# Where the weight stream lands: four raw buffers against the low halves of an eight-slot ring, in a two-layer decoder trunk

## The reference

```
xn = rmsnorm(h); q,k,v,cb,cc,cu,pu,gates = split(xn @ w_in)       # 1024 x 6656
att  = stick_breaking_attention(rmsnorm(q), rmsnorm(k), v)         # 8 heads x 64
conv = cb * causal_conv3(cc * cu);  pool = scale * group_linear(window_mean(pu) - pu)
h += (sum_j sigmoid(gates_j) * (branch_j @ w_branch_j)) @ w_out
h += peer(rmsnorm(h))        # 16384 one-neuron experts: top 16 of each of 8 heads
h += sigmoid(rmsnorm(h) @ w_ple_gate) * (p @ w_ple_proj)
```

## Time and profile before

| | us |
|---|---|
| median of 3 timed runs | 3993.78 (3993.38 to 3993.9) |
| the profiled execution | 3999.43 |
| its span, first to last instruction | 3997.5 |
| PE busy in it | 3923.6 |
| DVE busy | 2696.9 |
| ACT busy | 1453.8 |
| POOL busy | 1305.6 |

### The profile page before, as it was taken

The page is one execution under the profiler, slowest core; times in us unless marked ns, Lnnn a source line. Parts: engine busy times, 40 slices in busy tenths (PEclk is TensorE's granted clock), DMA queues, the critical chain, the costliest instruction groups (busy, mean ns, idle before and its releaser), DMA issues.

```text
span 3997.5 us, 57499 instructions
## 1 busy us (share of the span) xinstructions
PE 3923.6 (98%) x18154; PEld 3235.6 (81%) x18154; DVE 2696.9 (67%) x4417; ACT 1453.8 (36%) x1925; POOL 1305.6 (33%) x887
## 2 busy tenths in 40 slices
PE   8999999999999999999999999999999999999997
PEld 5777888888888878888767778888888888788886
DVE  6753649967774278778577546498777732888785
ACT  5433333333333333333444333333333333333334
POOL 1100003433331077666101000044333401767651
PEclk9999999999999999999999999999999999999999
DMA  3222223445454599999212223234445446999992
GB/s 112 74 84 90 100 86 129 147 161 187 173 184 147 192 338 367 353 350 346 106 68 75 89 90 106 80 137 145 172 176 189 169 147 206 348 371 357 353 332 74
DMA packets 323761, 740.32 MB, mean 185 GB/s; under 512 B 30496, under 2 KB 161696, under 8 KB 319904
## 3 DMA queue, kind: packets, MB, share of 16 engines
q1 hardware_dynamic: 104400, 381.73, 26.8%
q10 hardware_dynamic: 174160, 222.40, 16.5%
q0 software_dynamic: 45056, 134.38, 9.0%
HBM read 618.87 MB, written 119.54 MB: 185 GB/s over the span
## 4 chain that ended last, share of the span: by engine, by line
PE 94%; issue 2%; DVE 2%; ACT 1%; POOL 1%; DMA 0%; ACTq 0%; DVEq 0%; POOLq 0%; SPq 0%
PE bank L1180 61%; PE bank L1395 24%; PE bank L1375 4%; PE bank L1242 1%; PE bank L1232 1%; PE bank L1250 1%; ACT hi L439 0%; PE bank L1325 0%; PE bank L1324 0%; PE bank L1227 0%; PE bank L1323 0%; DVE xl L776 0%; DMA vrow<-in_stream,tail_v 0%; ACTq L645 0%; DVE lo L764 0%
## 5 line engine op out<-in xcount | busy, mean ns | idle before, releaser
L1180 PE MATMUL bank<-xh,hi 128*128 128x512 f32 x3264 | 1308.7, 401 | 24.4 <-DVE xl L776 18.7
L1180 PE MATMUL bank<-xh,lo 128*128 128x512 f32 x3264 | 1275.8, 391 | 0.0
L1180 PE MATMUL bank<-xl,hi 128*128 128x512 f32 x3264 | 1275.5, 391 | 0.0
L764 DVE TENSOR_TENSOR lo<-raw,hi 128x1024 fp32r<-128x1024 f32 (+1 forms) x532 | 645.3, 1213 | 520.3 <-ACT hi L439 485.7
L439 ACT ACTIVATE hi<-raw 128x1024 fp32r<-128x1024 f32 x724 | 739.7, 1042 | 318.9 <-DMA raw<-in_stream 188.0
L386 POOL TENSOR_TENSOR lo<-raw,hi 128x1024 fp32r<-128x1024 f32 x192 | 480.7, 2504 | 975.7 <-ACT hi L439 975.5
L1180 PEld LDWEIGHTS bank<-xh,hi 128*128 128x128 f32 x3264 | 616.2, 189 | 161.8 <-DVE xl L776 23.8
L1180 PEld LDWEIGHTS bank<-xh,lo 128*128 128x128 f32 x3264 | 614.8, 188 | 130.2
L1180 PEld LDWEIGHTS bank<-xl,hi 128*128 128x128 f32 x3264 | 616.7, 189 | 123.9 <-issue 5.6
L398 POOL DMA_INDIRECT hval<-early,tail_h x256 | 383.7, 1499 | 427.9 <-DMA early<-eo 347.2
L1395 PE MATMUL bank<-hi,ah 128*128 128x512 f32 x1536 | 476.0, 391 | 11.3 <-DVE al L1081 9.8
(11 more groups left out here) (209 smaller groups left out, 3512.1 us busy)
## 6 DMA issues: line engine op xcount, KB each, us to landing
raw<-in_stream SPq DMA_DIRECT2D x724, 512.0 KB
early<-eo ACTq DMA_DIRECT2D x256, 256.0 KB, 2.1
gate_table<-stage ACTq DMA_DIRECT2D x24, 2048.0 KB, 7.4
gb<-gate_table ACTq DMA_DIRECT2D x64, 768.0 KB
eb<-early ACTq DMA_DIRECT2D x64, 768.0 KB
hval<-early,tail_h POOLq DMA_INDIRECT x256
vrow<-in_stream,tail_v POOLq DMA_INDIRECT x256
hT<-in_xT ACTq DMA_DIRECT2D x2, 1024.0 KB, 8.3
```

What stands on the lines that cost most here:

```text
L764: dve.tensor_tensor(lo[k % RING][:, 0:w], raw[k % RAW][:, 0:w], hi[k % RING][:, 0:w].bitcast(f32), ALU.subtract).then_inc(lo_split, 1)
L1180: ins = pe.matmul(out_ap, st[slot][:, a:a + P], mv, start=first and i == 0, stop=last and i == 2)
```

## The change

The four raw buffers are gone. `raw[i]` becomes another name for the memory of `lo[i]`, so a tile lands in the place of its own low half, and the subtraction that makes `lo` writes over its own first operand. There are eight such places, each with its own landing semaphore. As PE reads `lo`, the load of tile n may not start before PE has done with tile n-8: SP waits for `tile_done` where it waited for `lo_split`, and the starting increment of 4 on `lo_split` goes away. ACT's wait on `tile_done` is kept. SP's loops are written out for pairs of groups, since the slot (0 to 3 or 4 to 7) now depends on the group. The order of the tiles in HBM and the work on PE, DVE, ACT and POOL stay as they are; 16 KB a partition are free and not used.

```diff
-RING, RAW, AHEAD = 8, 4, 4
+RING, AHEAD = 8, 4
...
-    raw = [sb(f"raw{i}", o_raw + 4 * KB * i, [P, 1024]) for i in range(RAW)]
     hi = [sb(f"hi{i}", o_ring + 8 * KB * i, [P, 1024], f32r) for i in range(RING)]
+    raw = [sb(f"raw{i}", o_ring + 8 * KB * i + 4 * KB, [P, 1024]) for i in range(RING)]
     lo = [sb(f"lo{i}", o_ring + 8 * KB * i + 4 * KB, [P, 1024], f32r) for i in range(RING)]
...
-            return l * T + i * 8 + k, l * (T // RAW) + i * 2 + k // RAW
+            return l * T + i * RING + k, l * (T // RING) + i + k // RING
...
-            def load(n, at):
-
-                for r in range(RAW):
-                    sp.wait_ge(lo_split, n + (r + 1))
-                    sp.dma_start(raw[r][:, :], stream[bass.ds(at + r, 1), :, :].rearrange("a p n -> (a p) n"))\
-                      .then_inc(raw_in[r], 16)
+            def load(n, at, slot):
+
+                for r in range(EG):
+                    sp.wait_ge(tile_done, n + (r + 1))
+                    sp.dma_start(raw[slot + r][:, :], stream[bass.ds(at + r, 1), :, :].rearrange("a p n -> (a p) n"))\
+                      .then_inc(raw_in[slot + r], 16)
...
                 with sp.Fori(0, EARLY - 1) as i:
                     for z in range(2):
-                        load(l * T + i * 8 + (N_V + z * EG), l * T + i * 12 + (X_ODD + EG + z * EG))
+                        load(l * T + i * 8 + (N_V + z * EG), l * T + i * 12 + (X_ODD + EG + z * EG), EG - z * EG)
...
-                    pool.tensor_tensor(lo[k % RING][:, :], raw[k % RAW][:, :], hi[k % RING][:, :].bitcast(f32),
+                    pool.tensor_tensor(lo[k % RING][:, :], raw[k % RING][:, :], hi[k % RING][:, :].bitcast(f32),
...
-            dve.sem_inc(lo_split, RAW)
...
-                dve.tensor_tensor(lo[k % RING][:, 0:w], raw[k % RAW][:, 0:w],
+                dve.tensor_tensor(lo[k % RING][:, 0:w], raw[k % RING][:, 0:w],
                                   hi[k % RING][:, 0:w].bitcast(f32), ALU.subtract).then_inc(lo_split, 1)
...
-                    pe.wait_ge(lo_split, RAW + l * T + i * 8 + k + 1)
+                    pe.wait_ge(lo_split, l * T + i * 8 + k + 1)
```

More of the change, by code:

```diff
@@ L136, in trunk_kernel @@
     KB = 1024
-    o_h, o_c, o_raw, o_ring, o_x = area(16 * KB), area(4 * KB), area(16 * KB), area(64 * KB), area(32 * KB)
+    o_h, o_c, o_ring, o_x = area(16 * KB), area(4 * KB), area(64 * KB), area(32 * KB)
     o_r, o_t, o_b = area(32 * KB), area(19 * KB), area(24 * KB)
@@ L249, in trunk_kernel @@
         x_in, vec_in, keys_in, out_done = [sem("x_in0"), sem("x_in1")], sem("vec_in"), sem("keys_in"), sem("out_done")
-        raw_in = [sem(f"raw_in{i}") for i in range(RAW)]
+        raw_in = [sem(f"raw_in{i}") for i in range(RING)]
         hi_split = sem("hi_split")
@@ L307, in _ @@
         def _(sp):
-            def load(n, at):
-                for r in range(RAW):
-                    sp.wait_ge(lo_split, n + (r + 1))
-                    sp.dma_start(raw[r][:, :], stream[bass.ds(at + r, 1), :, :].rearrange("a p n -> (a p) n"))\
-                      .then_inc(raw_in[r], 16)
-            with sp.Fori(0, DEPTH) as l:
[L317 to L322, removed]
+            def load(n, at, slot):
[3 more added lines that the diff above has]
+                      .then_inc(raw_in[slot + r], 16)
@@ new lines, in _ @@
+            with sp.Fori(0, DEPTH) as l:
+                with sp.Fori(0, X_ODD // RING) as i:
+                    for z in range(2):
+                        load(l * T + i * RING + z * EG, l * T + i * RING + z * EG, z * EG)
+                with sp.Fori(0, EARLY // 2) as i:
+                    for z in range(2):
+                        load(l * T + i * RING + (X_ODD + z * EG), l * T + i * 24 + (X_ODD + z * 12), z * EG)
+                load(l * T + (N_V - 3 * EG), l * T + (X_ODD + 12 * (EARLY - 1)), 0)
+                load(l * T + (N_V - 2 * EG), l * T + (X_END + 2 * EG), EG)
+                load(l * T + (N_V - EG), l * T + (X_END + 4 * EG), 0)
@@ L323, in _ @@
                 with sp.Fori(0, EARLY - 1) as i:
                     for z in range(2):
-                        load(l * T + i * 8 + (N_V + z * EG), l * T + i * 12 + (X_ODD + EG + z * EG))
+                        load(l * T + i * 8 + (N_V + z * EG), l * T + i * 12 + (X_ODD + EG + z * EG), EG - z * EG)
                 for z, at in enumerate((1, 3, 5, 6)):
-                    load(l * T + (N_V + (LAST_E + z) * EG), l * T + (X_END + at * EG))
-                with sp.Fori(0, (T - N_PT) // RAW) as i:
-                    load(l * T + i * RAW + N_PT, l * T + i * RAW + N_PT)
@@ L330, in _ @@
-            load(DEPTH * T, DEPTH * T)
+                    load(l * T + (N_V + (LAST_E + z) * EG), l * T + (X_END + at * EG), EG - z % 2 * EG)
+                for z in range((T - N_PT) // EG):
+                    load(l * T + (N_PT + z * EG), l * T + (N_PT + z * EG), EG - z % 2 * EG)
+            load(DEPTH * T, DEPTH * T, 0)
             sp.wait_ge(ple_added, 8 + DEPTH * DC)
@@ L436, in split @@
                 w = width(k)
-                act.wait_ge(raw_in[k % RAW], turn * 16 + 16)
+                act.wait_ge(raw_in[k % RING], turn * 16 + 16)
                 act.wait_ge(tile_done, n + 1)
-                act.activation(hi[k % RING][:, 0:w], raw[k % RAW][:, 0:w], ACT.Copy).then_inc(hi_split, 1)
+                act.activation(hi[k % RING][:, 0:w], raw[k % RING][:, 0:w], ACT.Copy).then_inc(hi_split, 1)
             def square(l, k, c):
@@ L1100, in period @@
                             low(i * 2 + z + 1, 1 - z)
-                dve.wait_ge(lo_split, RAW + l * T + N_U + POOL_E)
+                dve.wait_ge(lo_split, l * T + N_U + POOL_E)
                 apart(dve)
@@ L1283, in pair @@
                     pe.wait_ge(pooled_lo, s1 + 1)
-                    pe.wait_ge(lo_split, RAW + l * T + b * 8 + 8)
+                    pe.wait_ge(lo_split, l * T + b * 8 + 8)
                     three(bank[2][:, :], (7, 0), ph[:, :], pl[:, :], True, True).then_inc(tile_done, 1)
@@ L1301, in _ @@
                         if m % 2 == 0:
-                            pe.wait_ge(lo_split, RAW + l * T + k + 1)
+                            pe.wait_ge(lo_split, l * T + k + 1)
                         for c in range(GROUPS):
@@ L1390, in values @@
                         s = N_V + z * EG + k
-                        pe.wait_ge(lo_split, RAW + l * T + i * 8 + s + 1)
+                        pe.wait_ge(lo_split, l * T + i * 8 + s + 1)
                         for m in range(MT):
@@ L1408, in _ @@
                 values(NG // 2 - 1, 1, last=True)
-                pe.wait_ge(lo_split, RAW + l * T + N_PLE)
+                pe.wait_ge(lo_split, l * T + N_PLE)
                 def project(m):
```

4 lines of the change are left out of this document (2 added, 2 removed).

## The result

The kernel before took 3993.9 us (median of 17 runs, 3992.69 to 3997.12), the changed one 4001.29 us (17 runs, 3997.66 to 4005.38). The ratio is 1.0016, 95% interval 1.0009 to 1.0023: slower by 7.4 us, which is within the 0.2% called no change, though the interval lies clear of 1. The profiled execution after took 3998.72 us with a span of 3997.0, less than the 3999.43 and 3997.5 of before.

A forecast was written before the change was run, and what follows sets the result against it. PE bounds the kernel (94% of the chain), so moved loads show only where PE waits. Passage terms of 0.5 and 1.0 us sum to 1.5 a layer, 3.0 for two: median 3996.8, predicted 3997, range 3991 to 4006.

The forecast's parts named there:

- Instructions: All stages: instructions, loads and bytes stay in kind and number; a `lo` overwriting its own operand costs 0.
- Steady V costs 0: V's groups: loads start 5.3 and 2.1 us later, but 9.8 us of cover for `al` keeps this from PE.
- The passage: From U to V in each layer: sooner loads slow the transfers behind `al`, 1.5 us a layer, 3.0 for two.
- The load ahead of the last write of `early`: Passage: the load at 1396.5 delays the write of 1397.11 by 0 to 1.5 us; 0.5 taken.
- Group 2's loads against `hval`: Passage: the load at 1405.7, in the full stretch where `hval` lands, costs 0 to 1.8 us; 1.0 taken.
- Against the first `vrow`: Passage: the load at 1409.8 beside the first `vrow` gathers costs 0 to 1.8 us; 0 taken.
- The gain at POOL's second gather: Passage: the second `hval` gather, no longer beside the load of 1399.46, comes 0 to 1.1 us sooner; 0 taken.
- A longer pause has no more of the clock to lose: Passage: PE's clock already falls to mostly the 1.2 GHz level in this pause, so no term.
- Only the second has DMA in its chain: Of PE's two largest waits for DVE, `xl` (18.7 us) and `al` (9.8 us), only `al` has DMA in its chain.
- A: Passage: new loads delay the fetches, not the chain, so nothing reaches PE: 3993.8, or 3991.1 with gains; chance 0.17.
- B: V: long `eb` fetch issues, from 9 us on, stop ACT; 11 us if one group in four; 4005 or 4008; chance 0.14.
- C: Program start: new loads served beside the first make PE start up to 6 us later, 4002.8 with passages; chance 0.04.

The follow-up runs named there:

- e1: Changed kernel, but each load also waits for the `lo` of tile n-4 as before the change: 3995.11 us, ratio 1.0000.
- e12: e1 with DVE computing `al` and the four `lo` of group 1 ahead of its `hval` wait in V's first period: 3993.61 us, ratio 0.9997.
- e2: Changed kernel, with only the four loads of V's group 2 also held by the old `lo` wait: 4002.53 us, ratio 1.0018.
- e3: Changed kernel, with only the load of group 1's last tile also held by the old `lo` wait: 4001.36 us, ratio 1.0016.
- e4: Changed kernel, with only the load of query tile 83 also held by the old `lo` wait: 4000.09 us, ratio 1.0014.
- e7: Changed kernel, with DVE computing `al` and the four `lo` of group 1 ahead of its `hval` wait in V's first period: 3996.86 us, ratio 1.0006.
- e10: Changed kernel, DVE's first two V periods reordered so `al`, `lo` and group 2's `af` come ahead of gather-dependent work: 4000.56 us, ratio 1.0018.
- e8: e7 with the load of query tile 83 also held by the old `lo` wait: 3995.23 us, ratio 1.0003.
- e11: e10 with the load of query tile 83 also held by the old `lo` wait: 3995.14 us, ratio 1.0001.

## Why the prediction was right, and where it was not

The forecast was 3997 and no change, and the time is 4001.29: inside the range, 4.3 us above the figure. Of the rise of 7.4 us, 3.0 were in the sum. The direction and the place of the larger part were foreseen; that the time still lies in the range is in part luck, for the range was wide enough to take in a cost in the query stage that no term stood for. That the result is called no change rests on the 0.2% limit alone, which 7.4 us just keep.

**Instructions: right.** `lo` in place costs nothing, with both engines' rows and e1 for it. This is shown for the kernels before and after; e12 leaves a doubt only for a kernel without the pause.

**Steady V costs 0: right.** 489.60 in both layers of the changed kernel, twice profiled. The loads in group 24 of layer 1 moved as said, counted from the group's start: 5.4 and 2.2 us later. The landing of the first took longer than the 7.5 us allowed, about 9.2, and its `hi` was done with 2.0 us to spare before ACT's wait for PE ended. The cover, which I had left at 9.8 us, is smaller there. ACT's rows and DVE's after are

```profile
1799.74 4.28 ACTq L648 DMA_DIRECT2D eb<-early  x1
1804.14 2.98 ACT L442 ACTIVATE hi<-raw 128x1024 fp32r<-128x1024 f32 x3 [3.62 <-issue]
...
1805.23 1.23 DVE L766 TENSOR_TENSOR lo<-raw,hi 128x1024 fp32r<-128x1024 f32 x1 [3.63 <-ACT hi L442]
1806.38 1.75 DVE L1083 TENSOR_TENSOR al<-af,ah 128x1536 fp32r<-128x1536 f32 x1
```

The group starts at 1929.40 - 8 x 16.32 = 1798.84 and the next at 1815.16, so `al` is ready 7.0 us ahead of PE's need, where it was 9.8 us. DVE waits 3.63 us for a `hi`, and that stood behind the issue of `eb`, which took 4.28 us here and 1.51 in the same group before: the later loads are not what shortened the cover. Over groups 2 to 31 its median is 8.8 and 8.4 us in the two layers, before 9.3 and 8.8.

**The passage: right mechanism, the term too small.** I had 1.5 us a layer and it costs 2.50 and 3.13, above the 1.5 forecast and inside the 5.1 of the upper bounds. The terms fared as follows.

- The load ahead of the last write of `early`: I took 0.5 of 0 to 1.5. The write landed 4.1 us after its issue where it had landed after 2.0, so 2.1 later: outside the bounds. I had given the load's head start as a reason for little delay. It is the reverse: the write's packets start when most of the load's have started (the rows above). The bounds rested on 512 KB at 296 to 347 GB/s. But e2 shows that of this delay only 0.2 to 0.3 us reach `aval`.
- Group 2's loads against `hval`: I took 1.0 of 0 to 1.8; alone they cost `aval` 0.9 and 0.6 (e3), with the late write 1.8 and 2.4.
- Against the first `vrow`: I took 0, since `acc` waited 1.03 us for its row. It waits 1.92 now. That row was a wait that already was there, hence a chain without spare time, and the term should have had half of its bound. In e3, with the write on time, it waits 2.34 and 2.28: this term alone is 1.3 to 1.4 us.
- The gain at POOL's second gather: it took 2.02 us before; what gained was the distance from the first to the fourth gather, 5.0 us before and 4.4 after. It is real, 0.6 us, and lost in the rest.
- "A longer pause has no more of the clock to lose": right. Group 1 grew by 2.50 and 3.13 us while PE's wait grew by 2.6 and 3.2.

The Trainium skill's rule that I weighed ("DMA: Bandwidth & Descriptors", section "Queues, rings and completion order": turns between queues, packet by packet) I had read as an even share of small turns, by which the write is held back by its own size, 0.8 us. The trace does not show that: the write's packets start behind the load's, and it is 2.1 us late. That is nearer to the other case of the prediction, in which the queue that asked first is emptied first, with 1.5 us for the write. The sum of the even share, some 5 us for both layers, is near the 5.6 of the passages by chance. The misreading was mine. That section of the Trainium skill puts about 9 to 17 descriptors into one packet, and the load's 144 entries, which the profile calls packets, are 9 for each of 16 engines, so by an estimate from that figure the whole load is a single turn. With this reading the trace agrees. The section of the Trainium skill also says that a semaphore increment lands only after every earlier write of that DMA engine, across its queues. By that the load could hold back the report of the write. Here it need not: from 1399.5 on only packets of the write start, 60 of them, and it is reported at 1400.5. For the keys the load had landed at 501.95, 4.7 us before they did, so this rule doesn't explain their delay.

**The query stage: missed.** The step that failed is the sentence "Only the second has DMA in its chain". It was read from PE's two largest waits, and the row of `ql`, 0.6 us in two waits, stood further down the same view. Behind it is `keyh`, for which ACT waited 3.96 us on a landing. I looked at where loads move in V and at the passage, and not at where else the load of tile n ran into a transfer that something waits for. It is worth 0.4 to 1.9 us a layer; e4 shows it. It is a term that stood at nothing without a reason, and the start, which I had set aside as having no DMA in its chain, has a landing at its head as well.

**Rivals.** A (nothing reaches PE) fell by e1 against after. Its 0.5 us wait in layer 2 did go (0.8 us of V), but it is missing in e1 too. B did not happen in the changed kernel, whose longest `eb` issue is 7.5 us, but its mechanism is real: in e2 and e7 issues of 10.7 and 11.3 us stopped PE for 5.3 and 5.0 us, one of 9.6 in e10 for 4.7, and one of 10.0 in e8 for 0.8. Its point of some 9 us does not hold: 9.1 us in e1 and 10.3 in e11 stopped nothing, and 8.8 and 8.1 in e12 went with 5.4 and 3.0, 8.15 in e2 with 1.6. It depends on what the group has to spare. C (the start) did not happen: PE's first wait is 13.4 us as before.

**What stays open.** Why the keys take 1.4 us longer once they are under way, with the load landed; why the medians of e3 and e4 fall less than their stages (0 of 3.1 us and 1.2 of some 3.5); and what splits the cost at the passage between `hval` and `vrow` beyond the figures above, since no run held one of group 2's loads alone.

## What to carry to other kernels

A load that may start earlier will do so beside transfers that were alone, and what counts is not its own slack but theirs. Before freeing a buffer wait, list the transfers on which an engine waits within some microseconds of each load's new start, at each passage between stages, and read every row of waits that PE has, also those under 1 us. Where the old wait staggered loads behind the work that needed the queue, keep it as a wait on that work, even if memory no longer asks for it: e1 keeps the smaller footprint at no cost.

## What the runs showed of the hardware

A 512 KB load issued 0.5 to 1.0 us ahead of another queue's transfer went with a delay of 2.1 us in that one, at two unlike places, and e3 and e4, which hold the load back, undo it: the 256 KB write of `early` from 2.0 to 4.1 us, the 1 MB of keys from 4.9 to 7.0. At the write, the profile shows why: its packets start when 114 of the load's 144 have started, 2.5 us after the issue instead of 0.8. A mean busy share hides this (0.52 from 1396 to 1404 us, 0.85 from 1397.9 to 1399.8). Over all 256 writes of `early` the median went from 2.1 to 3.9 us, and of these only the last of each layer, for which POOL waits, comes into the time.

The issue of one `eb` fetch on ACT takes from 0.5 to 11.3 us, with the same bytes each time, and ACT's work behind it stands still meanwhile (`hi` 10.63 us behind the issue of 11.30 in e7).
